# Up projection of the first block: each of four modulation chunks stands three places later in the stream of transfers

## The reference, cut to what matters

```
mod = silu(c) @ w_ada + b_ada                  # 1024 -> 6 * 1024
shift1, scale1, gate1, shift2, scale2, gate2 = split(mod, 6)
...
h2 = modulate(rms_norm(x, g_norm2), shift2, scale2)
u  = causal_depthwise_conv(h2 @ w_up, w_conv, b_conv)   # 1024 -> 2 * 2816
val, gte = split(u, 2)
x  = x + (1 + gate2) * ((val * silu(gte)) @ w_down)     # 2816 -> 1024
```

## Time and profile before

| | us |
|---|---|
| Median of 3 runs | 1119.37 (1118.38 to 1119.7) |
| The profiled execution | 1115.07 |
| Its span in the trace | 1113.3 |
| PE busy | 1046.7 (94%) |
| DVE busy | 750.5 (67%) |
| ACT busy | 555.8 (50%) |
| Up projection of the first block, from its first matmul to the first of the down projection | 200.92 to 338.92 |

### The profile page before, as it was taken

How to read it: one execution, slowest core, us unless ns; L and a number is a source line. 1 busy time by engine, 2 the same in 40 slices (tenths; PEclk the granted TensorE clock), 3 DMA queues, 4 the chain that set the end, 5 groups by cost and what they waited for, 6 DMA issues and landing times.

```text
span 1113.3 us, 23986 instructions
## 1 busy us (share of the span) xinstructions
PE 1046.7 (94%) x10514; PEld 996.8 (90%) x10514; DVE 750.5 (67%) x1232; ACT 555.8 (50%) x828; POOL 0.9 (0%) x7
## 2 busy tenths in 40 slices
PE   4999999898989999998788999999999999999997
PEld 4988889898989998886668999999999799999996
DVE  6789668778887657977545555566666755555554
ACT  5245364654456548754233544444567645444441
POOL 0000000000000000000000000000000000000000
PEclk9989999999999999999999999999999999999999
DMA  8858455244465662422002555445514535554451
GB/s 353 326 217 320 166 213 206 97 190 189 190 250 188 207 234 98 152 79 77 5 3 77 189 190 190 154 155 184 180 62 134 190 114 190 190 190 154 157 183 39
DMA packets 30377, 185.90 MB, mean 167 GB/s; under 512 B 3376, under 2 KB 4672, under 8 KB 12864
## 3 DMA queue, kind: packets, MB, share of 16 engines
q1 hardware_dynamic: 30272, 184.36, 45.4%
HBM read 183.29 MB, written 1.05 MB: 166 GB/s over the span
## 4 chain that ended last, share of the span: by engine, by line
PE 76%; DVE 13%; DMA 4%; ACT 4%; issue 3%; SPq 0%; DVEq 0%; ACTq 0%
PE banks L355 40%; PE banks L1255 16%; DVE wlo L315 4%; PE banks L335 3%; DMA raw<-in_w_up 3%; PE banks L352 3%; ACT whi L300 2%; DVE adac L522 2%; DMA con<-in_cons 1%; DVE S L522 1%; PE banks L1792 1%; PE banks L575 1%; PE banks L1799 1%; DMA raw<-in_a_in 1%; PE banks L1782 1%
## 5 line engine op out<-in xcount | busy, mean ns | idle before, releaser
L315 DVE TENSOR_TENSOR wlo<-raw,whi 128x2048 fp32r<-128x2048 f32 (+3 forms) x167 | 332.2, 1990 | 195.7 <-ACT whi L300 195.4
L300 ACT ACTIVATE whi<-raw 128x2048 fp32r<-128x2048 f32 (+3 forms) x167 | 278.3, 1668 | 159.9 <-PE banks L1255 76.8
L355 PE MATMUL banks<-h_hi,whi 128*128 128x256 f32 x1424 | 190.6, 286 | 13.6 <-ACT whi L300 9.6
L355 PEld LDWEIGHTS banks<-h_hi,whi 128*128 128x128 f32 x1424 | 177.6, 191 | 18.9 <-issue 12.4
L355 PE MATMUL banks<-h_hi,wlo 128*128 128x256 f32 x1424 | 185.5, 282 | 0.2
L355 PE MATMUL banks<-h_lo,whi 128*128 128x256 f32 x1424 | 185.0, 281 | 0.0
L355 PEld LDWEIGHTS banks<-h_hi,wlo 128*128 128x128 f32 x1424 | 175.5, 190 | 2.4 <-issue 1.2
L355 PEld LDWEIGHTS banks<-h_lo,whi 128*128 128x128 f32 x1424 | 173.4, 188 | 3.1 <-issue 2.6
L1281 ACT ACTIVATE u<-u 128x256 f32<-128x256 f32 x44 | 18.4, 418 | 128.8 <-DVE u L1335 128.8
L1255 PE MATMUL banks<-m_lo,whi 128*128 128x256 f32 x528 | 75.0, 280 | 0.0
L1255 PE MATMUL banks<-m_hi,whi 128*128 128x256 f32 x528 | 74.9, 280 | 0.0
(11 more groups left out here) (449 smaller groups left out, 1377.6 us busy)
## 6 DMA issues: line engine op xcount, KB each, us to landing
raw<-in_ada SPq DMA_DIRECT2D x24, 1024.0 KB, 5.0
raw<-in_w_up SPq DMA_DIRECT2D x22, 1024.0 KB, 6.4
raw<-in_a_gu SPq DMA_DIRECT2D x22, 1024.0 KB, 4.8
raw<-in_b_gu SPq DMA_DIRECT2D x22, 1024.0 KB, 4.8
raw<-in_w_in SPq DMA_DIRECT2D x12, 1024.0 KB, 6.6
raw<-in_w_down SPq DMA_DIRECT2D x16, 704.0 KB, 4.2
raw<-in_a_in SPq DMA_DIRECT2D x11, 1024.0 KB, 5.1
raw<-in_a_down SPq DMA_DIRECT2D x16, 704.0 KB, 4.1
```

The source lines that it names most:

```text
L300: act.activation(hi_s[k % NSPLIT][:, 0:w], raw[n % NRAW][:, 0:w], ACT.Copy).then_inc(*hi_made.tick(k))
L315: dve.tensor_tensor(lo_s[s][:, 0:w], raw[n % NRAW][:, 0:w], hi_s[s][:, 0:w].bitcast(F), SUB).then_inc(*lo_made.tick(k))
L355: i_ = pe.matmul(b[0:m, j * T:(j + 1) * T], a[:, kt * step + j * m:kt * step + j * m + m], x[:, kt, :], start=st, stop=sp)
```

## The change

```diff
@@ -123,8 +123,8 @@
     for i in range(22):
         o.append(("w_up", i))
-        if i % 4 == 2 and i < 16:
-            o.append(("ada", 20 + i // 4))
+        if i % 4 == 1 and 4 < i < 18:
+            o.append(("ada", 19 + i // 4))
     for name in ("w_down", "a_in", "a_out", "a_gu", "a_down", "kv_down", "b_in",
```

## The result

| | before | after |
|---|---|---|
| Median, beside each other | 1118.88 us (4 runs) | 1107.59 us (4 runs) |
| Ratio, with its 95% interval | | 0.9883 (0.9861 to 0.9905) |
| The profiled execution | 1115.07 us | 1103.98 us |
| Its span | 1113.3 us | 1102.2 us |
| Stage: first matmul of U0 to the first of `w_down` | 138.0 us | 126.4 us |

The changed kernel is faster by 11.3 us in the medians, and by 13 (10.6 to 15.6) as the ratio has it.

What follows compares the result with a forecast made beforehand. PE, busy 94% of the span, was taken as the bound, standing still where SP's blocked queue delayed weight transfers. Savings of 4.60, 2.33 and 3.35 us sum to 10.28, taking 1119.37 to 1109.1 us; range 1106.0 to 1113.0.

Steps and rivals of the forecast that it cites:

- What bounds the stage: First block's up projection: PE waits at U10, U14, U18 because SP, held by modulation chunks, issues `w_up` transfers late.
- Transfers in the new order: Up projection: U6 issued about 213.5, landings near the 6.4 us median, late transfers costed at nothing.
- DVE in the new order: Up projection: after a modulation chunk DVE's taps start 3.5, 2.4, 1.3 us behind PE, then in step again.
- the cover: Up projection: DVE's latest low part done 7.3 us after PE's chunk end, wanted at 13.1, leaving 5.8 us.
- What PE gets back: Up projection: waits and slowed passes at U10, U14, U18 give 4.60, 2.33 and 3.35, together 10.28 us.
- At U10 ... Together 4.60: PE at U10: 2.98 us of wait plus 1.33 and 0.29 of slowed passes won back.
- The clock: PE's passes after the gaps: saving not one number, 8.9 us with no slow pass, about 13 with one per gap.
- Behind the stage: Down projection and after: work and waits only move along, costed at nothing; a few later stalls may meet the clock differently.
- part of the gain: Up projection: buffers stay the bound, only U10's stall goes, 4.6 us won, 1114.8 us; chance 0.07.
- no change: Up projection: DVE's own load makes PE wait as long as now, 1119.4 us; chance 0.03.
- Late: Up projection: modulation chunks land too late for DVE, up to 1131.5 us at 28 us landings; chance 0.02.
- More slow passes than the profiled run shows: PE passes behind the three gaps: larger gain of about 13 us, 1106.4 us; chance 0.08.

Runs made afterwards that it cites:

- taking U6's away alone: Kernel before with only the first modulation chunk's transfer, A20, moved to behind U5; A21 to A23 left in place: 1116.71 us, ratio 0.9952.
- leaving it alone: Kernel before with A21, A22 and A23 moved three places later and A20 left behind U2: 1108.22 us, ratio 0.9879.
- second trace of before: The kernel before, unaltered, run and traced again: 1120.0 us in one run, stage 138.45 us.
- third trace: Kernel before with only two small transfers moved from in front of chunk 3 of `a_in` to chunk 4: 1119.48 us, ratio 0.9988.
- three groups: The follow-up kernels' timing sets, each beside the kernel before on one chip; before had medians of 1122.5, 1121.2 and 1120.8 us.
- six places: Modulation chunks' transfers six places later than in the kernel before, behind U8, U12, U16, U20: 1125.16 us, ratio 1.0037.
- five places later: Modulation chunks' transfers five places later than in the kernel before, behind U7, U11, U15, U19: 1108.96 us, ratio 0.9886.
- the work moved: Transfer list of the kernel before; DVE takes A20 to A23 earlier, in loops 0, 4, 8, 12, and PE's sums move too: 1108.57 us, ratio 0.9888.
- the last with both edits: Changed kernel plus two small transfers moved to in front of chunk 4 of `a_in`, timed beside the changed kernel: 1107.92 us, ratio 0.9882.

## Why the prediction was right in its mechanism and off in one term

- *What bounds the stage*: right. The three waits of PE are gone, and with them ACT's waits for transfers of `w_up`. That U6's lateness, invisible to PE, set up U10's is shown from both sides: taking U6's away alone removed U10's wait, and leaving it alone was free once nothing was blocked behind it.
- *Transfers in the new order*: right. U6 issued 12.3 us behind PE's start of the stage (12.6 forecast); landings near 5 us. That those of 12.3 us came from joint issues was an assumption; the trace of before bears it out, with 4.8 us for the first of the four issued within 1.3 us and 12.3 for the last, and the longest is 5.5 in the new order.
- *DVE in the new order*: right to 0.2 us (3.7, 2.5, 1.4 for 3.5, 2.4, 1.3), and the cover held.
- *What PE gets back*: this is the step that failed, in its term "At U10 ... Together 4.60". In the second trace of before the same term measures 5.5 us (3.89 of wait, 1.48 and 0.14 of slow passes), and in the third 6.9 (4.13, 1.68 and 1.08). The wait had been measured from where PE stood in the first trace, and PE stood there 0.96 us later than need be (18 passes of 1.92 instead of 1.87). While a transfer sets the end of a wait, slow passes ahead of it are hidden in it; when the wait goes, their speed counts. The changed kernel ran those passes at 1.87, so the whole wait of 3.9 was there to be won. With 0.96 more the sum is 11.2 and not 10.28. From the start of U1 to the down projection the traces give 11.3 (130.69 before, 119.41 after).
- *What came out as forecast by its making, and by chance*: from U7 to the down projection the changed kernel took 85.45 us (243.30 to 328.75) against 85.6 forecast. The forecast is the first trace's 95.9 less 10.28, and the 0.96 us lie ahead of U7, so this sign could not show the error. (The 95.9 of before runs to 339.08, a time of the chain; in the timeline of PE the down projection starts at 338.92.) Its first matmul came at 328.75 for 328.8 forecast by chance: the stage began 1.45 us later and was 1.3 us shorter than forecast.
- *The stage*: from the start of U0 it shrank by 11.6 us. The 0.3 above the 11.3 are U0, 6.97 us instead of 7.31 (202.37 to 209.34 against 200.92 to 208.23). The change doesn't touch U0: it took 6.97 to 8.48 us in the nine traces in which PE never waits behind it.
- *The clock*: the saving isn't one number, as said. The three traces with the old list and the work in its old places have stages of 138.0, 138.5 and 140.6 us; the nine in which PE never waits behind U0 have 126.4 to 128.9. Without U0, from the start of U1, these are 130.7, 130.6 and 133.4 against 119.4 in six traces and 120.2 to 120.5 in three whose passes take up to 1.89 us. So the change wins 11.2 us where one pass of those three chunks is slow, and 14.0 where three are (3.55, 2.95 and 3.41 us in the third trace). By the Trainium skill, "TensorE: Matmul & The Clock Gate", section "Part 1: The HAM clock gate", the number of slow matmuls varies from run to run of one kernel. The traces agree in part: the two of the unaltered kernel have one slow first pass in three gaps each, the third, of the same code up to there, two in three.
- *From the profiled execution to the median*: the sum was read from an execution of 1115.07 us, 4.3 under the median, and these 4.3 us were taken to be no part of the saving. Over the whole execution its granted clock was 0.988. In the three groups the executions of before have medians of 0.981 and 0.982, and those of the kernels without a wait in the stage 0.983 to 0.987. So before runs at a lower clock in the median than in the execution that was read, and the change gives some of that back. No run shows how much of it lies in this stage; the second trace of before, at 1120.0 us, is 4.9 us longer than the first, with a stage only 0.4 longer.
- *Behind the stage*: right in kind. Before the stage the changed profile is 1.45 us later and behind it 0.9 shorter: 1.45 - 11.6 - 0.9 = -11.1, the difference of the spans. The first goes with the granted clock, which was 0.95 and 0.94 in the two windows between 120 and 150 us, where it was 1.00 before. So does the second: between 498 and 518 us it was 0.91 before, and 1.00 in the same work after.
- *The rivals*: "part of the gain" and "no change" fall with the trace. "Late" is what six places do, not three. "More slow passes than the profiled run shows", with a gain of 13, is not excluded: the seven ratios of kernels whose only edit is in the list or in the place of `dve_ada`, and that have no wait in the stage, run from 0.9879 to 0.9906, so 10.5 to 13.6 us, with a mean of 12.4. Single intervals reach down to 8 us, but all seven lie above the forecast. About 1 us of the difference is the term at U10; that the rest is slow passes fits the third trace and is not shown, since only one execution of each kernel timed is traced.

## What to carry to other kernels

In a ring of buffers with one in-order issuer, list the transfers in the order in which the engines free the buffers, or at most so far from it that each held issue still lands before its use: here one, three and five places later won all, and six lost it again. A late transfer may cost nothing where it is seen and still cost at the next one; look for the backlog that it leaves. And read a wait's length from more than one trace, since what runs slowly ahead of it is hidden in it.

## What the hardware showed that I had not expected

- Passes of 16 identical matmuls have more than one level at full granted clock, from 1.87 to 1.92 us (0.117 to 0.120 per matmul). In the first trace of before the level was 1.92 until the four one-column matmuls behind U6 and 1.87 from then on the earlier trace rows; in the second trace of it, and in the changed kernel, it was 1.87 from U1. With five places later it was 1.89 from U1 to the end of the stage, and in two other traces (the work moved, and the last with both edits) it went up from 1.87 to 1.89 behind the first group of one-column matmuls. No run here shows what sets it.
- A 1 MB transfer of `w_up` lands in 4.8 us (median) in the changed kernel, where the issues of the stage are 3.3 us or more apart. In the kernel before, with four issues within 1.3 us from 228.49 on, the first landed in 4.8 us and the last in 12.3.
- The gap of PE at U18 was 2.7 to 2.9 us in all four traces that had it, so its length alone doesn't tell whether the clock falls. In two of them the pass behind it was slow (2.66 and 3.30, then 2.91 and 3.57 us of idle and pass as listed), in two it wasn't (2.72 and 2.11, 2.80 and 2.11).
